# A two-block transformer kernel: SBUF tensors laid out anew, masked_bias apart from the tiles of attention "a"

## The chip, the cores and the metric

One core of one Trainium2 chip. The metric is the device time of one execution in microseconds (us); lower is better.

## The reference

512 tokens of 1,024 features, fp32, pass through two blocks. Block one: RMS norm, one wide projection (`h @ w_in`), windowed grouped-query attention "a" (8 query heads, 2 key heads, window 128, ALiBi slopes and a sink), neighbourhood attention "b" on an 8 x 64 grid with a relative bias, gates, output projection, and an MLP of 4,096 with squared ReLU. Block two has two layers, each a SwiGLU MLP of 2,816, a mixer (sliding-window attention "c" beside a short convolution), and a second SwiGLU MLP. A last RMS norm ends it. For attention "b":

```python
bias = rpb_f[:, dr[:, None, None], dc[None, :, :]]
sc = sc + jnp.transpose(bias, (0, 2, 1, 3))[None]
p = jax.nn.softmax(sc.reshape(b, h, GRID_W, kh * B_KW), axis=-1)
```

and for the MLPs:

```python
x = x + jnp.square(jax.nn.relu(h2 @ w_up[l])) @ w_down[l]          # block one
(jax.nn.silu(h @ w_gate) * (h @ w_up)) @ w_down                     # block two, twice per layer
```

## The kernel before

All activations lie transposed in SBUF, features on the 128 partitions and the 512 tokens along them, in tiles of 2 KB per partition. Each fp32 product is made of three matmuls in fp32r: the high part of the weights by the high part of the activation (L758), high by low (L759), low by high (L760). A weight unit is 128 rows of up to 1,024 columns; three are held (`w_raw`, `w_hi`, `w_lo`). The load queue on SyncE fetches a unit (L1385), ScalarE casts it to `w_hi` (L870), and VectorE (L1066) or, during the attentions, GpSimd (L1305) makes `w_lo`, the rest. A unit feeds eight steps of three matmuls. Results leave PSUM through VectorE into a ring of five `z` tiles, or onto `x`.

A planner writes one list of jobs; each engine walks that list in order and takes its own part of each job, with waits on semaphores between engines. So an engine's queue order is the list's order. Attention steps (score, turn, multiply, turn_out) are set between the dense steps at slots counted by the planner. `split_g` is a weight split on GpSimd, `mask_bias` a job of GpSimd that makes from `rel_bias` the masked bias of attention "b" (affine selects, L1348); VectorE adds it to the scores (L1223). The mask jobs of block 0 stand behind `finish_beside()`, which runs out all steps of attention "a".

SBUF tensors are allocated one after the other in the order of the code, each at a multiple of 32 bytes. Tensors of a stage are allocated on an inner stack and share their space with those of other stages: `act_hi`, `act_lo`, `rms_first` with the mixer's tiles, and within the first mixer the tiles of `part_a` (`ka_hi`, `ka_lo`, `va`) with those of `part_b` (`masked_bias`, `gates_a`). The first tensor of the kernel starts at byte 16,512 of a partition. The small constants come first, then a filler of 256 bytes named `to_page`, so that `x` starts at byte 20,480 (five times 4,096); `h_hi` and `h_lo` (16 KB each), the nine weight buffers (4 KB each), three row sums and the ring follow, then the stages' tiles. Constants in question: `identity` at 16,512, `ones` at 17,024, `dist_1` at 17,536; `dist_2` at 188,448, `masked_bias` at 215,040.

The job and its wait, which the change touches:

```python
pool.wait_ge(in_landed["bias"].s, 16 * BLOCK_C)
if i == 0:
    pool.wait_ge(*done("multiplied", ("a", BLOCKS - 1, 1, len(CHUNKS["a"][BLOCKS - 1]) - 1)))
else:
    pool.wait_ge(*done("biased", ("b", i - 1, g, GROUP - 1)))
```

Of the kernel before, what the change touches and what calls it, by code (L numbers as in the profile page):

```python
# [6 lines left out]
F32 = mybir.dt.float32  # L7
F32R = mybir.dt.float32r
# [4 lines left out]
P = 128  # L13
TOKENS = 512
D_MODEL = 1024
HEAD = 64
HEADS = 8
KV_HEADS = 2
GROUP = HEADS // KV_HEADS
BLOCK = 128  # L20
BLOCKS = TOKENS // BLOCK
KT = D_MODEL // P
# [8 lines left out]
UNIT = KT * P  # L31
UNITS_HELD = 3
Z_RING = 5
# [21 lines left out]
def whole_chunks(windows):  # L55
    return [[(s // BLOCK + c, c * BLOCK, BLOCK) for c in range(n // BLOCK)] for s, n in windows]
# [3 lines left out]
CHUNKS = {"a": whole_chunks(WINDOW_1), "c0": whole_chunks(WINDOW_2), "c1": whole_chunks(WINDOW_2),  # L60
          "b": [[(i, 0, CHUNKS_VB[i][1]), (i + 1, CHUNKS_VB[i][1], CHUNKS_VB[i + 1][1])] for i in range(BLOCKS)]}
# [469 lines left out]
def two_blocks(nc, dram, out):  # L531
    stack = ExitStack()
    with stack:
        def sbuf(name, shape, dt=F32, on=stack):
            return on.enter_context(nc.sbuf_tensor(name, shape, dt))

        def signal(name, step=1):
            return Signal(stack.enter_context(nc.semaphore(name)), step)

        identity = sbuf("identity", [P, P])  # L540
        ones = sbuf("ones", [P, P])
        dist_1 = sbuf("dist_1", [P, 3 * BLOCK])
# [11 lines left out]
        sink_exp = sbuf("sink_exp", [P, 2, HEADS])  # L554
        row_sum = sbuf("row_sum", [P, 2, HEADS])
        row_inv = sbuf("row_inv", [P, 2, HEADS])
        sbuf("to_page", [P, 64])

        x = sbuf("x", [P, KT, TOKENS])
        h_hi = sbuf("h_hi", [P, KT, TOKENS], F32R)  # L560
        h_lo = sbuf("h_lo", [P, KT, TOKENS], F32R)
        w_raw = [sbuf(f"w_raw{i}", [P, UNIT]) for i in range(UNITS_HELD)]
        w_hi = [sbuf(f"w_hi{i}", [P, UNIT], F32R) for i in range(UNITS_HELD)]
        w_lo = [sbuf(f"w_lo{i}", [P, UNIT], F32R) for i in range(UNITS_HELD)]
        scaled_sum = sbuf("scaled_sum", [P, TOKENS])
        rms_inv = sbuf("rms_inv", [P, TOKENS])
        square_sum = sbuf("square_sum", [P, TOKENS])
        z = [sbuf(f"z{i}", [P, TOKENS]) for i in range(Z_RING)]


        with ExitStack() as on:
            act_hi = sbuf("act_hi", [P, FF_RING, TOKENS], F32R, on)
            act_lo = sbuf("act_lo", [P, FF_RING, TOKENS], F32R, on)
            rms_first = sbuf("rms_first", [P, TOKENS], F32, on)
        with ExitStack() as on:
            qa = sbuf("qa", [P, HEADS, TOKENS], F32R, on)
            qb_hi = sbuf("qb_hi", [P, 4, TOKENS], F32R, on)
            qb_lo = sbuf("qb_lo", [P, 4, TOKENS], F32R, on)
            probs_t1 = sbuf("probs_t1", [P, 2, TOKENS], F32, on)
            out_q1 = sbuf("out_q1", [P, TOKENS], F32, on)  # L580
            probs_1 = sbuf("probs_1", [P, 3, GROUP, 3 * BLOCK], F32, on)
            with ExitStack() as kv_part:
                kb_hi = sbuf("kb_hi", [P, 4, TOKENS], F32R, kv_part)
                kb_lo = sbuf("kb_lo", [P, 4, TOKENS], F32R, kv_part)
                vb = sbuf("vb", [P, BLOCKS + 1, HEADS, HEAD], F32, kv_part)
                rel_bias = sbuf("rel_bias", [P, HEADS, 2 * BLOCK], F32, kv_part)
                with ExitStack() as part_a:
                    ka_hi = sbuf("ka_hi", [P, KV_HEADS, TOKENS], F32R, part_a)
                    ka_lo = sbuf("ka_lo", [P, TOKENS], F32R, part_a)
                    va = sbuf("va", [P, BLOCKS, KV_HEADS, HEAD], F32, part_a)  # L590
                with ExitStack() as part_b:
                    masked_bias = sbuf("masked_bias", [P, HEADS, 2 * BLOCK], F32, part_b)
                    gates_a = sbuf("gates_a", [P, 2, TOKENS], F32, part_b)
            with ExitStack() as part_m:
                mg_hi = sbuf("mg_hi", [P, KT, TOKENS], F32R, part_m)
                mg_lo = sbuf("mg_lo", [P, KT, TOKENS], F32R, part_m)
                gates_b = sbuf("gates_b", [P, 2, TOKENS], F32, part_m)
        with ExitStack() as on:
            q2 = sbuf("q2", [P, HEADS, TOKENS], F32R, on)
            k2_hi = sbuf("k2_hi", [P, KV_HEADS, TOKENS], F32R, on)  # L600
            k2_lo = sbuf("k2_lo", [P, TOKENS], F32R, on)
            v2 = sbuf("v2", [P, BLOCKS, KV_HEADS, HEAD], F32, on)
            probs_t2 = sbuf("probs_t2", [P, 2, TOKENS], F32, on)
            out_q2 = sbuf("out_q2", [P, TOKENS], F32, on)
            probs_2 = sbuf("probs_2", [P, 3, GROUP, 2 * BLOCK], F32, on)
            cv_hi = sbuf("cv_hi", [P, 4, TOKENS], F32R, on)
            cv_lo = sbuf("cv_lo", [P, 4, TOKENS], F32R, on)
            conv_c = sbuf("conv_c", [P, TOKENS], F32, on)
            conv_y = sbuf("conv_y", [P, TOKENS], F32, on)
            conv_u = sbuf("conv_u", [P, TOKENS + 2], F32, on)  # L610
            dist_2 = sbuf("dist_2", [P, 2 * BLOCK], F32, on)

        bank = [stack.enter_context(nc.psum_tensor(f"bank{i}", [P, TOKENS], F32)) for i in range(8)]
        dense_bank, score_bank, turn_bank, value_bank = bank[0:4], bank[3:5], bank[5:7], bank[7]
# [15 lines left out]
        done = plan.value  # L630
# [668 lines left out]
        def gpsimd_program(engine):  # L1299
            pool = Once(engine)  # L1300
            for job, key, r, zs in jobs:
# [32 lines left out]
                elif job == "mask_bias":  # L1334
                    i, g = key
                    first, lower, upper = {0: (HALF_BLOCK // GRID_R, (8, 24), (24, 32)), 1: (0, (0, 32), (0, 32)),
                                           3: (0, (0, 8), (8, 24))}[i]
                    heads = lambda t, a, b: t[:, 4 * g:4 * g + 4, :].rearrange("p h (j r) -> p h j r", r=GRID_R)[:, :, a:b, :]
                    pool.wait_ge(in_landed["bias"].s, 16 * BLOCK_C)
                    if i == 0:  # L1340
                        pool.wait_ge(*done("multiplied", ("a", BLOCKS - 1, 1, len(CHUNKS["a"][BLOCKS - 1]) - 1)))
                    else:
                        pool.wait_ge(*done("biased", ("b", i - 1, g, GROUP - 1)))
                    for (a, b), sign, base, event in ((lower, 1, GRID_R - 1, "bias_half"), (upper, -1, (WIN_W - 1) * GRID_R, "bias_masked")):
                        in_place = i == 1 and sign < 0
                        if sign < 0:
                            pool.wait_ge(*done("bias_half", key))
                        engine.affine_select(out=heads(masked_bias, a - first, b - first),  # L1348
                                             in_=heads(masked_bias, a, b) if in_place else heads(rel_bias, a, b),
                                             compare_op=ALU.is_ge, fill=-MASKED, base=base + sign * GRID_R * a,  # L1350
                                             pattern=[[0, 4], [sign * GRID_R, b - a], [0, GRID_R]], channel_multiplier=-sign).then_inc(signals[event].s, 1)

                elif job == "merge_b":
                    m = key
                    pool.wait_ge(*done("merged", m))
                    engine.dma_start(x[:, m, :], dram["x"][m * P:(m + 1) * P, :]).then_inc(x_back[m].s, 16)

                elif job == "conv_h":
                    layer, f = key
                    pool.wait_ge(*done("evacuated", r))  # L1360
                    if f > 0:
                        pool.wait_ge(*done("conv_back_2", (layer, f - 1)))
                    engine.tensor_tensor(conv_u[:, 2:TOKENS + 2], z[zs % Z_RING][:, :], conv_c[:, :], ALU.mult).then_inc(signals["conv_u"].s, 1)

                elif job == "conv_b":
                    pool.wait_ge(*done("evacuated", r))
                    pool.wait_ge(*done("conv_back_2", key))
                    engine.tensor_tensor(z[zs % Z_RING][:, :], z[zs % Z_RING][:, :], conv_y[:, :], ALU.mult).then_inc(signals["conv_out"].s, 1)

                elif job == "output":  # L1370
                    for n, cols in enumerate(halves):
                        pool.wait_ge(signals["inverted"].s, n + 1)
                        for m in output_order:
                            if m < WITH_GAIN:
                                pool.wait_ge(*done("x_gained", m))
                                engine.tensor_tensor(x[:, m, cols], x[:, m, cols], rms_inv[:, cols], ALU.mult).then_inc(signals["output_scaled"].s, 1)
# [181 lines left out]
```

## Time and profile before

| | |
|---|---|
| median of 3 runs | 2581.93 us (2581.85 to 2585.58) |
| profiled execution | 2581.85 us, span 2580.1 us |
| TensorE busy (matmul) | 2543.6 us |
| VectorE, ScalarE, GpSimd busy | 1232.9, 886.2, 276.3 us |
| DMA | 235.36 MB, mean 91 GB/s |

Engines in the rows: PE is TensorE's matmuls, PEld its weight loads, DVE VectorE, ACT ScalarE, POOL GpSimd, SP SyncE. L12 is line 12 of the kernel. Busy time of PE is modelled, since matmuls overlap; the distance between their starts tells the rate. "idle before <- X" is time in which the engine stood still ahead of the instruction, and what ended it.

### The profile page before, as it was taken

The page shows a single profiled execution, that of the slowest core. Times are in us where ns is not written, and L with a number is a line of the kernel's source. Part 1 is how long each engine was busy: PE and PEld are TensorE (multiplying, and loading weights), DVE is VectorE, ACT ScalarE, POOL GpSimd, SP SyncE. Part 2 cuts the span into 40 slices and gives each one's busy share as a digit, 9 for nine tenths or more (in the row PEclk, how much of TensorE's full clock was granted, in tenths as well). Part 3 has the DMA queues.
Part 4 walks back from the last instruction along what each step waited for, and adds up shares of the span by engine and source line. Part 5 has one row for each costly group of instructions (what it writes and reads, how often), then busy time and mean ns, then how long its engine had stood idle before and what let it go on. Part 6 is the DMA issues. An engine that isn't in the chain of part 4 may idle for free.

```text
span 2580.1 us, 28068 instructions
## 1 busy us (share of the span) xinstructions
PE 2543.6 (99%) x11494; PEld 2079.2 (81%) x11494; DVE 1232.9 (48%) x1518; ACT 886.2 (34%) x1329; POOL 276.3 (11%) x194
## 2 busy tenths in 40 slices
PE   7999999999999999999999999999999999999997
PEld 6777888888888888877888888888888778888886
DVE  5444455334465343455454444543434644544444
ACT  4445434223353222344332222422223443322222
POOL 4233110000030000013300000100000132000002
PEclk9999999999999999999999999999999999999999
DMA  5111232333323333231223232333332312233322
GB/s 163 50 50 52 91 116 93 98 99 97 98 83 106 98 98 98 82 100 58 78 94 101 95 98 92 96 98 98 98 98 82 100 59 78 94 100 95 99 94 69
DMA packets 69424, 235.36 MB, mean 91 GB/s; under 512 B 8753, under 2 KB 11441, under 8 KB 69297
## 3 DMA queue, kind: packets, MB, share of 16 engines
q1 hardware_dynamic: 67632, 230.36, 28.2%
q0 software_dynamic: 1664, 3.22, 0.6%
q8 instruction: 91, 1.49, 0.2%
q14 instruction: 37, 0.30, 0.0%
HBM read 231.35 MB, written 2.19 MB: 91 GB/s over the span
## 4 chain that ended last, share of the span: by engine, by line
PE 90%; DVE 4%; ACT 2%; issue 2%; POOL 0%; DMA 0%; SPq 0%; DVEq 0%; ACTq 0%; POOLq 0%
PE bank L758 29%; PE bank L760 28%; PE bank L759 28%; PE bank L772 2%; PE bank L799 2%; DVE w_lo L1066 2%; PE bank L786 1%; ACT w_hi L870 1%; DVE x L1167 1%; ACT z L861 0%; POOL square_sum L1315 0%; DVE q L1123 0%; DVE z L1058 0%; PE bank L810 0%; PE bank L832 0%
## 5 line engine op out<-in xcount | busy, mean ns | idle before, releaser
L758 PE MATMUL bank<-h_hi,w_hi 128*128 128x512 f32 x2224 | 893.0, 402 | 11.2 <-DVE w_lo L1066 9.7
L760 PE MATMUL bank<-h_hi,w_lo 128*128 128x512 f32 x2224 | 869.1, 391 | 0.0
L759 PE MATMUL bank<-h_lo,w_hi 128*128 128x512 f32 x2224 | 868.8, 391 | 0.0
L1066 DVE TENSOR_TENSOR w_lo<-w_raw,w_hi 128x1024 fp32r<-128x1024 f32 (+1 forms) x387 | 483.9, 1251 | 327.0 <-ACT w_hi L870 326.7
L870 ACT ACTIVATE w_hi<-w_raw 128x1024 fp32r<-128x1024 f32 (+1 forms) x438 | 451.9, 1034 | 414.8 <-PE bank L760 412.9
L758 PEld LDWEIGHTS bank<-h_hi,w_hi 128*128 128x128 f32 x2224 | 418.6, 188 | 109.8 <-DVE w_lo L1066 11.2
L760 PEld LDWEIGHTS bank<-h_hi,w_lo 128*128 128x128 f32 x2224 | 418.5, 188 | 88.6
L759 PEld LDWEIGHTS bank<-h_lo,w_hi 128*128 128x128 f32 x2224 | 419.2, 189 | 81.1 <-issue 1.9
L758 PE MATMUL bank<-act_hi,w_hi 128*128 128x512 f32 x960 | 373.9, 389 | 0.0
L760 PE MATMUL bank<-act_hi,w_lo 128*128 128x512 f32 x960 | 373.9, 389 | 0.0
L759 PE MATMUL bank<-act_lo,w_hi 128*128 128x512 f32 x960 | 373.9, 389 | 0.0
L1058 DVE TENSOR_TENSOR z<-bank,rms_inv 128x512 f32<-128x512 f32 x238 | 168.5, 709 | 301.6 <-PE bank L760 300.8
L1315 POOL TENSOR_TENSOR square_sum<-square_sum,z 128x512 f32<-128x512 f32 x62 | 83.9, 1353 | 1853.3 <-ACT z L861 1852.3
L1167 DVE SCALAR_TENSOR_TENSOR x<-bank,x 128x512 f32<-128x512 f32 x152 | 104.7, 689 | 281.8 <-PE bank L760 281.7
L759 PEld LDWEIGHTS bank<-act_lo,w_hi 128*128 128x128 f32 x960 | 180.3, 188 | 37.4
L758 PEld LDWEIGHTS bank<-act_hi,w_hi 128*128 128x128 f32 x960 | 180.2, 188 | 37.4
L760 PEld LDWEIGHTS bank<-act_hi,w_lo 128*128 128x128 f32 x960 | 180.2, 188 | 37.2
L984 ACT ACTIVATE act_hi<-z 128x512 fp32r<-128x512 f32 x88 | 55.6, 632 | 389.6 <-DVE z L1188 389.6
L979 ACT ACTIVATE z<-z 128x512 f32<-128x512 f32 x88 | 55.6, 632 | 285.3 <-DVE z L1058 285.3
L1305 POOL TENSOR_TENSOR w_lo<-w_raw,w_hi 128x1024 fp32r<-128x1024 f32 x51 | 121.9, 2391 | 291.6 <-ACT w_hi L870 291.6
L1066 DVE TENSOR_TENSOR act_lo<-z,act_hi 128x512 fp32r<-128x512 f32 x120 | 83.2, 693 | 105.0 <-ACT act_hi L984 61.4
L1228 DVE SCALAR_TENSOR_TENSOR probs<-dist,bank 128x256 f32<-128x256 f32 (+2 forms) x96 | 40.4, 421 | 109.2 <-PE bank L772 109.2
(163 smaller groups left out, 1666.3 us busy)
## 6 DMA issues: line engine op xcount, KB each, us to landing
w_raw<-ffn_wg_dram SPq DMA_DIRECT2D x88, 512.0 KB, 3.5
w_raw<-ffn_wu_dram SPq DMA_DIRECT2D x88, 512.0 KB, 3.5
w_raw<-w_in_dram SPq DMA_DIRECT2D x70, 512.0 KB, 3.6
w_raw<-ffn_wd_dram SPq DMA_DIRECT2D x64, 512.0 KB, 3.5
w_raw<-w_up_dram SPq DMA_DIRECT2D x32, 512.0 KB, 3.5
w_raw<-w_down_dram SPq DMA_DIRECT2D x32, 512.0 KB, 3.8
w_raw<-w_out_dram SPq DMA_DIRECT2D x24, 512.0 KB, 3.5
w_raw<-ffn_wd_dram SPq DMA_DIRECT2D x32, 384.0 KB, 3.1
```

The lines of the kernel that those rows point to most:

```text
L758: engine.matmul(to, w_hi[s][:, lhs], hi, start=k == 0, stop=False)
L759: engine.matmul(to, w_hi[s][:, lhs], lo, start=False, stop=False)
L760: product = engine.matmul(to, w_lo[s][:, lhs], hi, start=False, stop=job == "k_last")
L772: product = engine.matmul(score_bank[at % 2][:, 0:count], q[:, block(i)], k[:, start:start + count], start=m == 0, stop=m == len(pairs) - 1)
L870: engine.activation(w_hi[s][:, 0:width], w_raw[s][:, 0:width], ACT.Copy).then_inc(signals["w_hi"].s, 1)
L979: engine.activation(z[zs[1] % Z_RING][:, :], z[zs[0] % Z_RING][:, :], ACT.Silu).then_inc(signals["silued"].s, 1)
L984: engine.activation(act_hi[:, plan.hidden[key] % FF_RING, :], z[zs[1] % Z_RING][:, :], ACT.Copy).then_inc(signals["act_hi"].s, 1)
L1058: engine.tensor_tensor(to, src, scale, ALU.mult).then_inc(signals["evacuated"].s, 1)
L1066: engine.tensor_tensor(lo, value, hi.bitcast(F32), ALU.subtract).then_inc(signals[event].s, 1)
L1167: engine.scalar_tensor_tensor(x[:, m, :], dense_bank[plan.results[r].bank][:, :], factor(r), x[:, m, :], ALU.mult, ALU.add).then_inc(signa ...
L1305: engine.tensor_tensor(w_lo[s][:, 0:width], w_raw[s][:, 0:width], w_hi[s][:, 0:width].bitcast(F32), ALU.subtract).then_inc(signals["w_lo_g ...
L1315: engine.tensor_tensor(to, to, z[zs % Z_RING][:, :], ALU.add).then_inc(signals["scaled_sum" if scaled else "square_sum"].s, 1)
```

## The change

Three things change. (1) The tensors that all stages use are allocated first, and the constants behind them; the filler `to_page` is gone, `scaled_sum` moves to the MLP's stage, and in the second mixer `dist_2` stands behind `q2` and `conv_u` ahead of `conv_y`. (2) `masked_bias` moves out of `part_b` and has space of its own beside the tiles of attention "a". (3) The wait of the mask job for the last value product of attention "a" is dropped. All instructions and their order stay; almost all addresses change.

```diff
+        x = sbuf("x", [P, KT, TOKENS])
+        h_hi = sbuf("h_hi", [P, KT, TOKENS], F32R)
+        h_lo = sbuf("h_lo", [P, KT, TOKENS], F32R)
+        w_raw = [sbuf(f"w_raw{i}", [P, UNIT]) for i in range(UNITS_HELD)]
+        w_hi = [sbuf(f"w_hi{i}", [P, UNIT], F32R) for i in range(UNITS_HELD)]
+        w_lo = [sbuf(f"w_lo{i}", [P, UNIT], F32R) for i in range(UNITS_HELD)]
+        rms_inv = sbuf("rms_inv", [P, TOKENS])
+        square_sum = sbuf("square_sum", [P, TOKENS])
+        z = [sbuf(f"z{i}", [P, TOKENS]) for i in range(Z_RING)]
         identity = sbuf("identity", [P, P])
         ones = sbuf("ones", [P, P])
         dist_1 = sbuf("dist_1", [P, 3 * BLOCK])
...
         row_inv = sbuf("row_inv", [P, 2, HEADS])
-        sbuf("to_page", [P, 64])
-
-        x = sbuf("x", [P, KT, TOKENS])
...
-        scaled_sum = sbuf("scaled_sum", [P, TOKENS])
-        rms_inv = sbuf("rms_inv", [P, TOKENS])
-        square_sum = sbuf("square_sum", [P, TOKENS])
-        z = [sbuf(f"z{i}", [P, TOKENS]) for i in range(Z_RING)]
...
             act_lo = sbuf("act_lo", [P, FF_RING, TOKENS], F32R, on)
+            scaled_sum = sbuf("scaled_sum", [P, TOKENS], F32, on)
             rms_first = sbuf("rms_first", [P, TOKENS], F32, on)
...
                 rel_bias = sbuf("rel_bias", [P, HEADS, 2 * BLOCK], F32, kv_part)
+                masked_bias = sbuf("masked_bias", [P, HEADS, 2 * BLOCK], F32, kv_part)
...
                 with ExitStack() as part_b:
-                    masked_bias = sbuf("masked_bias", [P, HEADS, 2 * BLOCK], F32, part_b)
                     gates_a = sbuf("gates_a", [P, 2, TOKENS], F32, part_b)
...
             q2 = sbuf("q2", [P, HEADS, TOKENS], F32R, on)
+            dist_2 = sbuf("dist_2", [P, 2 * BLOCK], F32, on)
...
             conv_c = sbuf("conv_c", [P, TOKENS], F32, on)
+            conv_u = sbuf("conv_u", [P, TOKENS + 2], F32, on)
             conv_y = sbuf("conv_y", [P, TOKENS], F32, on)
-            conv_u = sbuf("conv_u", [P, TOKENS + 2], F32, on)
-            dist_2 = sbuf("dist_2", [P, 2 * BLOCK], F32, on)
...
                     pool.wait_ge(in_landed["bias"].s, 16 * BLOCK_C)
-                    if i == 0:
-                        pool.wait_ge(*done("multiplied", ("a", BLOCKS - 1, 1, len(CHUNKS["a"][BLOCKS - 1]) - 1)))
-                    else:
+                    if i > 0:
                         pool.wait_ge(*done("biased", ("b", i - 1, g, GROUP - 1)))
```

## Rows read from the trace of the kernel before

**Rows 1.** The page: busy us, share of the span, instructions

```profile
PE 2543.6 (99%) x11494; PEld 2079.2 (81%) x11494; DVE 1232.9 (48%) x1518; ACT 886.2 (34%) x1329; POOL 276.3 (11%) x194
```

**Rows 2.** Windows: us, busy us by engine, granted clock, DMA share, GB/s

```profile
0.00:20.00 20.00, 10.27 (x33) 7.40 (x34) 12.54 (x13) 13.63 (x20) 6.23 (x8) 1.00 0.77 279
...
755.00:1080.00 325.00, 325.00 (x1436) 269.18 (x1435) 155.75 (x174) 90.87 (x109) 0.00 (x0) 1.00 0.30 95
```

**Rows 3.** Waits of TensorE, first and last of seven: us, times, longest

```profile
PE bank L758 <- DVE w_lo L1066: 9.7, 3, 8.6
...
PE bank L844 <- ACT z L861: 0.6, 1, 0.6
```

**Rows 4.** Timeline of TensorE in an MLP: start us, us

```profile
904.49 0.39 PE L759 MATMUL bank<-h_lo,w_hi 128*128 128x512 f32 x1
...
905.17 0.39 PE L759 MATMUL bank<-h_lo,w_hi 128*128 128x512 f32 x1
```

**Rows 5.** The page: a group, busy us, mean ns, idle before

```profile
L870 ACT ACTIVATE w_hi<-w_raw 128x1024 fp32r<-128x1024 f32 (+1 forms) x438 | 451.9, 1034 | 414.8 <-PE bank L760 412.9
```

**Rows 6.** Line 759 from 755 to 1080 us: ns min/median/max

```profile
L759 PE MATMUL bank<-h_lo,w_hi x342: 388/390/390, 754.9 to 1073.8; 128*128 128x512 f32 x171
L759 PEld LDWEIGHTS bank<-h_lo,w_hi x341: 187/188/188, 755.3 to 1073.6; 128*128 128x128 f32 x171
...
L759 PE MATMUL bank<-act_lo,w_hi x137: 388/390/390, 846.0 to 1079.9; 128*128 128x512 f32 x137
```

**Rows 7.** Timeline of TensorE at the end of attention "a"

```profile
165.44 0.60 PE L786 MATMUL bank<-identity,probs 128*128 128x128 f32 x4
...
170.69 1.00 PE L799 MATMUL bank<-va,probs_t 128*128 128x64 f32 x8
```

**Rows 8.** Timeline of GpSimd and VectorE around the first mask

```profile
175.93 2.40 POOL L1305 TENSOR_TENSOR w_lo<-w_raw,w_hi 128x1024 fp32r<-128x1024 f32 x1 [5.27 <-ACT w_hi L870]
178.28 4.14 POOL L1348 TENSOR_SCALAR_AFFINE_SELECT masked_bias<-rel_bias 128x512 f32<-128x512 f32 x4
...
180.71 0.36 DVE L1223 SCALAR_TENSOR_TENSOR probs<-bank,masked_bias 128x192 f32<-128x192 f32 x1 [1.83 <-POOL masked_bias L1348]
```

**Rows 9.** Groups by form, score plus masked bias

```profile
L1223 DVE SCALAR_TENSOR_TENSOR probs<-bank,masked_bias 128x256 f32<-128x256 f32 x16 | 6.8, 425 | 24.3 <-PE bank L772 24.3
```

**Rows 10.** Tile dist (dist_1 and dist_2): ns min/median/max

```profile
L1228 DVE SCALAR_TENSOR_TENSOR probs<-dist,bank x96: 286/422/556, 56.8 to 2142.0; 128x256 f32<-128x256 f32 x64, 128x384 f32<-128x384 f32 x16, 128x128 f32<-128x128 f32 x16
```

**Rows 11.** Tile conv_u, the two VectorE lines that read it

```profile
L1205 DVE SCALAR_TENSOR_TENSOR conv_y<-conv_u,conv_w,conv_y x8: 741/744/752, 1163.7 to 2156.3; 128x512 f32<-128x512 f32 x8
L1208 DVE SCALAR_TENSOR_TENSOR conv_y<-conv_u,conv_w,conv_y x8: 752/752/752, 1164.4 to 2157.1; 128x512 f32<-128x512 f32 x8
```

**Rows 12.** Line 832, the norm's product with ones

```profile
L832 PEld LDWEIGHTS bank<-square_sum,ones x16: 185/188/193, 26.0 to 2207.9; 128*128 128x128 f32 x16
L832 PE MATMUL bank<-square_sum,ones x16: 590/594/668, 26.2 to 2208.3; 128*128 128x512 f32 x16
```

**Rows 13.** Timeline in an MLP: a fetch, and the cast that reads it

```profile
898.61 0.33 SPq L1385 DMA_DIRECT2D w_raw<-ffn_wg_dram  x1
...
913.32 1.04 ACT L870 ACTIVATE w_hi<-w_raw 128x1024 fp32r<-128x1024 f32 x1
```

**Rows 14.** DMA issues: count, KB each, median us to landing

```profile
w_raw<-ffn_wg_dram SPq DMA_DIRECT2D x88, 512.0 KB, 3.5
...
w_raw<-ffn_wd_dram SPq DMA_DIRECT2D x32, 384.0 KB, 3.1
...
out_dram<-x SPq DMA_DIRECT2D x8, 256.0 KB, 2.4
...
dist<-dist_dram SPq DMA_DIRECT2D x2, 128.0 KB, 2.1
```

**Rows 15.** Timeline of the start: the third unit's cast

```profile
10.66 1.06 ACT L870 ACTIVATE w_hi<-w_raw 128x1024 fp32r<-128x1024 f32 x1 [0.18 <-DMA w_raw<-w_in_dram]
```

More of the change, by code:

```diff
@@ L556, in two_blocks @@
         row_inv = sbuf("row_inv", [P, 2, HEADS])
-        sbuf("to_page", [P, 64])
-        x = sbuf("x", [P, KT, TOKENS])
[L560 to L564, printed above, removed]
-        scaled_sum = sbuf("scaled_sum", [P, TOKENS])
-        rms_inv = sbuf("rms_inv", [P, TOKENS])
-        square_sum = sbuf("square_sum", [P, TOKENS])
-        z = [sbuf(f"z{i}", [P, TOKENS]) for i in range(Z_RING)]
         with ExitStack() as on:
```

## The prediction

> **What bounds the kernel now.** I read the first two parts of the page first. TensorE is busy 2543.6 us of a span of 2580.1 us, and VectorE, the next engine, is busy 48% [rows 1]. The windows by stage come next: in the second block's stretch of dense matmuls from 755 to 1080 us TensorE is busy 325.00 us of 325.00 at a granted clock of 1.00, so nothing but its own rate counts there, while in the first 20 us it is busy 10.27 us and DMA 0.77 [rows 2]. Then the waits of TensorE: the seven named ones add up to 21.4 us, from 9.7 (the start) down to 0.6 [rows 3]. So there are three places where time can move: TensorE's rate per matmul (some 2,500 us hang on it), these 21 us, and the ends of the kernel, where TensorE has no work.
>
> The rate is the place to look at closely, since the change is mostly one of addresses. Matmuls 0 and 3 of a run start at 904.49 and 905.17 us: 0.68 / 3 = 0.227 us apart [rows 4]. The 438 weight units [rows 5] feed eight steps of three matmuls each, or six steps for the 32 units of 384 KB [rows 14]: 3 x (406 x 8 + 32 x 6) = 10,320 matmuls. The reader is to see that it doesn't matter which operand a matmul reads: over h_lo the model's duration is 388/390/390 ns at least/median/most, over act_lo it is 388/390/390 [rows 6].
>
> **Part 1, the wait that goes.** The mask job of block 0 no longer waits for the last value product of attention "a". That product is the group of eight at 170.69 us, 1.00 us long, so it is over at 171.69 [rows 7]. GpSimd starts the selects at 178.28 us. What stands ahead of them in its queue is a weight split from 175.93 us, 2.40 us long: it ends at 178.33, and the selects begin with no idle time before them [rows 8]. The wait was fulfilled 6.6 us before GpSimd came to it. Taking it away lets nothing start earlier: GpSimd walks its jobs in order, and the job order is the same. I take 0. The lower bound is what a mask at time zero would free: VectorE idles 1.83 us for it, once [rows 8]. So the bounds are -1.8 and 0 us. A loss is excluded, since an instruction that waited for a fulfilled semaphore is only gone.
>
> **Part 2, masked_bias gets its own 8 KB.** Its writers and readers are the same, in the same order. It used to lie on ka_hi, ka_lo and va; now these three move up by 8 KB and gates_a (first written by the gate of tile 0) lies on ka_hi instead. The code already makes that gate wait for the last outputs of "a", which come after every read of ka_hi; that wait stands there before and after the change. If it were ever to bind, the gate behind it would stop ScalarE's casts, which have the 11 us of cover worked out below. 0 us.
>
> **Part 3, scaled_sum, dist_2 and conv_u move within their stages.** No wait in the code is added or taken away for them. dist_2 now lies inside the space of act_hi; its load already waits, in both kernels, for the last matmul of the MLP before. Behind it in the load queue stand weight fetches, as before. 0 us.
>
> **Part 4, every address.** Worked out from the sizes in the code: before, x starts at byte 20,480 of a partition, five times 4,096, and each of h_hi, h_lo, the nine weight buffers, the z ring, act_hi and act_lo starts at a multiple of 2,048. After, x starts at 16,512 = 4 x 4,096 + 128, and h, weights and z lie 128 bytes past such multiples; act_hi starts at 120,576, a multiple of 256 and of no more. The question is whether an engine or a DMA is slower (or faster) for that. The trace of before has operands off the 2,048 grid:
>
> - VectorE: dist_1 lies at 17,536 and dist_2 at 188,448 (128 and 32 past a multiple of 256), masked_bias at 215,040, a multiple of 2,048. A 128x256 scalar-tensor-tensor with one PSUM operand takes 425 ns with masked_bias; the 96 on the two dist tiles have a median of 422 [rows 9, 10]. conv_u is read 4 bytes past its start in 744 ns, at its start in 752 [rows 11]. No price.
> - ScalarE and GpSimd: I have no row for them off the grid and take VectorE's 0. They have cover: ScalarE is idle 414.8 us ahead of the casts [rows 5], GpSimd is busy 11% of the span [rows 1].
> - TensorE weight loads: ones lies at 17,024, 128 past a multiple of 256, exactly where the weights now go. Its loads take 185/188/193 ns; those of the weights on the grid 187/188/188 [rows 6, 12]. No price.
> - TensorE moving operand: no 512-column fp32r operand lies off the grid, so the trace doesn't have this case. The nearest is identity, at 16,512: 128 columns as moving operand of the transposes, four in 0.60 us [rows 7], that is (0.60 - 0.27) / 3 = 0.11 us apart. At the pace of the aligned product with ones (594 ns for 512 columns) [rows 12], 128 columns would take 0.15 us. So no slower than aligned. I take 0, and bound it at half a nanosecond per matmul either way (the spread between 388 and 390 is as large): 10,320 x 0.5 ns = 5.2 us.
> - Weight loads by DMA: a refill is issued at 898.61 us and read by the third cast after that (three slots in turn), at 913.32 us. That leaves 14.7 us for a landing that takes 3.5 us, so 11 us of cover [rows 13, 14]. Of ScalarE's 414.8 idle us ahead of the casts 412.9 end with a matmul, not with a DMA [rows 5]. If that cover were gone, a later landing would be paid on all 438 units.
> - The start, where this cover isn't there: the cast of the third unit begins at 10.66 us, after 0.18 us of waiting for its DMA, and TensorE's first groups wait for such casts and their rests (9.7 us in three waits) [rows 3, 15].
>
> What a DMA to an address off the grid costs: dist_2, 128 KB to 32 past a multiple of 256, lands in 2.1 us. Loads on the grid land in 3.5 us for 512 KB and 3.1 for 384 [rows 14], so 0.4 us per 128 KB, and 128 KB should take 2.3. It takes no more than that. I take 0; the upper bound is one 256-byte piece in sixteen more at the start, 1/16 of 10.66 us = 0.7 us, and at the end a quarter more of the moving part of one 256 KB store, 0.25 x 0.8 = 0.2 us of its 2.4 [rows 14].
>
> The Trainium skill (DMA: Bandwidth & Descriptors, How a descriptor splits into AXI transactions) speaks against this change: a descriptor is cut into 256-byte transactions, and one that doesn't start at a multiple of 256 needs one more. By that rule each 4,096-byte row of a weight buffer would take 17 transactions for 16, if it holds for the side that is written, and the whole change would come to about 2582.8 us. The landing of dist_2 shows no such price for written rows, and the stores at the end, which read x, will show the other side. By it, the weight refills would land some 0.1 us later with no one waiting.
>
> **The sum.** 2581.85 us (the profiled execution, whose span is 2580.1; the median of the three runs is 2581.93) + 0 + 0 + 0 + 0 = 2581.9 us. Below 0.2% of the time, 5.2 us, this kernel's measurement can't tell a change from none: its three runs lie up to 3.7 us apart.
>
> **Rivals.**
> - *The moving operand is streamed at another pace off the grid, slower* (the other side). One cycle more of the 2.4 GHz level per matmul is 0.42 ns x 10,320 = 4.3 us: 2586.2, still "same". It decides from 0.5 ns on; two cycles are 8.6 us: 2590.5 us. For it: this case is in no row, and 512 columns at 2.4 GHz are 213 ns where 227 are spent, so 14 ns have another cause, which may depend on the address. Against it: h_lo, act_lo, and each of their 2 KB-spaced tiles have one pace, and every new start is still a multiple of 128 bytes. 8 in 100.
> - *The same, but faster*: before, weights, x and h all start on the same 4,096 grid, and if part of the 14 ns is engines and DMA meeting at like addresses, spreading them gives some back. 4% of 14 ns = 0.56 ns, 5.8 us: 2576.1 us. Against it: VectorE, ScalarE and DMA come and go beside TensorE, and the pace stays at 0.227. 9 in 100.
> - *The mask wait mattered after all*: 1.8 us less, 2580.1 us, "same". 5 in 100, the queue order excludes it.
> - *DMA off the grid costs at the start and the end*: 0.7 + 0.2 = 0.9 us more, 2582.8 us, "same". 13 in 100.
> - No change anywhere: 65 in 100, the forecast.
>
> **How the numbers follow.** Same: 65 + 5 + 13 = 83 in 100, less 3 for spread between measurements that I give to the two sides: 0.80. Faster 9 + 2 = 0.11, slower 8 + 1 = 0.09. The range takes in the bounds of the hidden costs and the half nanosecond: 2581.9 - 5.2 and 2581.9 + 5.2, rounded, 2577 to 2587 us; about 2 in 10 is left outside.
>
> **What the profile after would show.** If right: spacing of dense matmuls 0.227 us, model durations 390, window of the MLP full; the selects again right behind the split near 175.93 us; weight landings at 3.5 us; the third cast near 10.66 us; VectorE's split still 1.23 us. It would be wrong if the TensorE spacing changed by half a nanosecond, if ScalarE's casts waited for DMA in the MLPs, or if VectorE's or GpSimd's operations got longer by enough that TensorE's 21.4 us of waits grew by a quarter.

## The result, and the profile after

The changed kernel takes 2604.16 us (median of 4 runs, 2604.01 to 2606.43), the kernel before 2583.76 us in the runs beside it (2581.85 to 2586.89). The ratio is 1.008 with a 95% interval of 1.0062 to 1.0097: slower by 0.8%, some 20 us. The prediction said 2581.9 us and no change, with 2577 to 2587 us as its range. The profiled execution took 2604.31 us, span 2602.5 us, 22.4 us over the 2580.1 us of the kernel before.

The page after, part 1 (busy us, share, instructions), answers to [rows 1], and its groups to [rows 5]:

```profile
PE 2567.8 (99%) x11494; PEld 2079.9 (80%) x11494; DVE 1232.8 (47%) x1518; ACT 886.6 (34%) x1329; POOL 276.8 (11%) x194
...
L868 ACT ACTIVATE w_hi<-w_raw 128x1024 fp32r<-128x1024 f32 (+1 forms) x438 | 452.0, 1034 | 431.0 <-PE bank L758 428.4
```

Every engine but TensorE has the busy time that it had, within half a microsecond. TensorE's grew by 24.2 us with the same 11,494 instructions. ScalarE's casts idle more, 431.0 for 414.8 us, and still all but 2.6 us of it ends with a matmul: ScalarE waits longer because TensorE is slower. So the time is in TensorE's own pace, and the groups of the same page say in which matmuls (mean ns behind the busy us):

```profile
L758 PE MATMUL bank<-h_hi,w_lo 128*128 128x512 f32 x2224 | 869.4, 391 | 0.0
L757 PE MATMUL bank<-h_lo,w_hi 128*128 128x512 f32 x2224 | 868.8, 391 | 0.0
...
L758 PE MATMUL bank<-act_hi,w_lo 128*128 128x512 f32 x960 | 379.2, 395 | 0.0
L756 PE MATMUL bank<-act_hi,w_hi 128*128 128x512 f32 x960 | 379.2, 395 | 0.0
L757 PE MATMUL bank<-act_lo,w_hi 128*128 128x512 f32 x960 | 379.1, 395 | 0.0
```

Those that read h have their 391 ns. Those that read act (the tiles `act_hi` and `act_lo`) went to 395 from the 389 that all three groups have on the page before, one of them:

```profile
L759 PE MATMUL bank<-act_lo,w_hi 128*128 128x512 f32 x960 | 373.9, 389 | 0.0
```

The durations are modelled, so the starts have to confirm it. Timeline of TensorE after, in a product with act (start us, us), beside [rows 4]:

```profile
992.15 0.39 PE L756 MATMUL bank<-act_hi,w_hi 128*128 128x512 f32 x1
992.38 0.40 PE L757 MATMUL bank<-act_lo,w_hi 128*128 128x512 f32 x1
992.62 0.39 PE L758 MATMUL bank<-act_hi,w_lo 128*128 128x512 f32 x1
992.85 0.40 PE L756 MATMUL bank<-act_hi,w_hi 128*128 128x512 f32 x1
...
994.95 0.39 PE L756 MATMUL bank<-act_hi,w_hi 128*128 128x512 f32 x1
```

From 992.15 to 994.95 there are 12 matmuls: 0.233 us each, where the kernel before has 0.227. Over all dense matmuls of the trace that follow one another at the upper clock level, the pace on act goes in turns, 229 and 237 ns, one matmul after the other, whatever the operand; the mean from start to start is 233.3 ns (226.7 before), and 227.1 on h in both kernels. All other tensors of a stage (q2, cv, mg, qb) went the way of act: 233.2 ns over all 3,648 matmuls on stage tensors, for 226.8 before. 3,648 x 6.4 ns = 23.3 us, and the loss is 22.4 us.

A small part of the 22.4 us has another cause. Windows of the kernel before, then of the one after (the third number from the end is the granted clock):

```profile
50.00:75.00 25.00, 21.53 (x84) 15.23 (x83) 13.42 (x22) 10.19 (x21) 7.19 (x3) 0.86 0.24 78
50.00:75.00 25.00, 21.52 (x75) 15.10 (x74) 12.38 (x19) 9.70 (x20) 7.21 (x3) 0.80 0.20 65
```

The clock was at its lower level for longer in this execution: 25 us x 0.06 = 1.5 us. It leaves some 21 us for the pace, so the sum of 23.3 us is a little high. The runs below say where such a sum runs high.

The mask, the part of the change that looked like the point of it, did nothing. Timelines of GpSimd and VectorE after, beside [rows 8]:

```profile
177.70 2.40 POOL L1303 TENSOR_TENSOR w_lo<-w_raw,w_hi 128x1024 fp32r<-128x1024 f32 x1 [5.28 <-ACT w_hi L868]
180.05 4.14 POOL L1344 TENSOR_SCALAR_AFFINE_SELECT masked_bias<-rel_bias 128x512 f32<-128x512 f32 x4
...
182.48 0.36 DVE L1221 SCALAR_TENSOR_TENSOR probs<-bank,masked_bias 128x192 f32<-128x192 f32 x1 [1.83 <-POOL masked_bias L1344]
```

The selects stand right behind the split, 2.35 us after its start as before, and VectorE's 1.83 us of waiting is there to the last digit; all is 1.8 us later, most of it the 1.5 us of clock above, which lie ahead of it.

### The profile page after: what moved, and what is told of

It reads as the page before. It is cut to its first block, busy times and chain, and to the rows that moved or that the text cites. A ratio compares the mean times of both kernels' runs of the same rounds, so it can differ in the third digit from the quotient of the medians.

```text
span 2602.5 us, 28067 instructions
## 1 busy us (share of the span) xinstructions
PE 2567.8 (99%) x11494; PEld 2079.9 (80%) x11494; DVE 1232.8 (47%) x1518; ACT 886.6 (34%) x1329; POOL 276.8 (11%) x194
## 4 chain that ended last, share of the span: by engine, by line
PE 92%; DVE 4%; ACT 2%; issue 1%; DMA 0%; POOL 0%; SPq 0%; DVEq 0%; ACTq 0%
PE bank L756 29%; PE bank L758 28%; PE bank L757 28%; PE bank L770 2%; PE bank L797 2%; DVE w_lo L1064 1%; PE bank L784 1%; ACT w_hi L868 1%; DVE x L1165 1%; ACT z L859 0%; DVE q L1121 0%; DVE z L1056 0%; PE bank L808 0%; DMA w_raw<-w_in_dram 0%; PE bank L830 0%
## 5 line engine op out<-in xcount | busy, mean ns | idle before, releaser
L868 ACT ACTIVATE w_hi<-w_raw 128x1024 fp32r<-128x1024 f32 (+1 forms) x438 | 452.0, 1034 | 431.0 <-PE bank L758 428.4
L758 PE MATMUL bank<-act_hi,w_lo 128*128 128x512 f32 x960 | 379.2, 395 | 0.0
L756 PE MATMUL bank<-act_hi,w_hi 128*128 128x512 f32 x960 | 379.2, 395 | 0.0
```

What stands on the lines that cost most here:

```text
L756: engine.matmul(to, w_hi[s][:, lhs], hi, start=k == 0, stop=False)
L758: product = engine.matmul(to, w_lo[s][:, lhs], hi, start=False, stop=job == "k_last")
L868: engine.activation(w_hi[s][:, 0:width], w_raw[s][:, 0:width], ACT.Copy).then_inc(signals["w_hi"].s, 1)
```

## The experiments

The theories, after the result. **O** (own address): a moving operand that starts off some grid streams more slowly. **R** (relation): the pace depends on the distance, the start of the moving operand less that of the weights. Worked out from the layout: before, every moving operand of a dense matmul and every weight buffer start at multiples of 256 bytes, distance 0 modulo 256. After, h is 128 past such a multiple and so are the weights (distance 0), act_hi starts at 120,576 and w_hi at 77,952: distance 42,624 = 166.5 x 256, so 128. What came between them are the 3,712 bytes of constants, 14.5 x 256. **W**: the dropped wait or the separate masked_bias.

**The whole change, with 128 bytes of constants ahead of x.**

```diff
+        gate_bias = sbuf("gate_bias", [P, 2 * KT])
+        eps_col = sbuf("eps_col", [P, 1])
+        root_ready = sbuf("root_ready", [P, 1])
         x = sbuf("x", [P, KT, TOKENS])
...
         dist_1 = sbuf("dist_1", [P, 3 * BLOCK])
-        eps_col = sbuf("eps_col", [P, 1])
-        root_ready = sbuf("root_ready", [P, 1])
...
-        gate_bias = sbuf("gate_bias", [P, 2 * KT])
```

> The whole change, but with 128 bytes of constants put ahead of x, so that x, h, the weights and z start 256 bytes past a multiple of 512, as the stage tensors (act_hi, act_lo, q2, cv, mg) do in the changed kernel. The stage tensors keep their addresses. Theory R (relation: the pace of a matmul depends on where its moving operand and the weights start relative to each other): all matmuls at 0.227 us, about 2582 us. Theory O (own address: a moving operand that starts 256 past a multiple of 512 is slow by itself): act stays at 233 ns and h joins it, 10,320 x 6.6 ns = 68 us over the kernel before, about 2650 us. Theory W (the dropped wait or the separate masked_bias did it): 2604 us as the changed kernel.

Measured: ratio to the kernel before 1.0001 (0.9991 to 1.001), median 2588.04 beside 2587.48 us (that the kernel before stands at 2587 us here, and at 2584 above, goes with the clock: see the last section). act keeps the very addresses that it has in the changed kernel and runs at the pace of before. Its groups:

```profile
L757 PE MATMUL bank<-h_lo,w_hi 128*128 128x512 f32 x2224 | 869.6, 391 | 0.0
L756 PE MATMUL bank<-act_hi,w_hi 128*128 128x512 f32 x960 | 373.4, 389 | 0.0
L757 PE MATMUL bank<-act_lo,w_hi 128*128 128x512 f32 x960 | 373.4, 389 | 0.0
```

W falls: the wait is gone, masked_bias is apart, and nothing is slower. O falls. R stands.

**256 bytes ahead of the stage tensors of the kernel before.**

```diff
         z = [sbuf(f"z{i}", [P, TOKENS]) for i in range(Z_RING)]
+        sbuf("to_stage", [P, 64])
```

> The kernel before with 256 bytes of filler ahead of the stage tensors: weights and h on the grid, act and the other stage tensors 256 past a multiple of 512; wait and masked_bias as before. Theory O: act at 233 ns, h at 226.7, some 2604 us. Theory R: act slow too, by an amount that depends on the distance (256 here, 128 in the changed kernel); fast only if distances count modulo 256. Theory W: 2582 us, no change.

Measured: ratio 0.9998 (0.9986 to 1.001), act 226.7 ns from start to start. Distance 256 costs nothing.

**512 bytes for 256 ahead of x in the kernel before.**

```diff
-        sbuf("to_page", [P, 64])
+        sbuf("to_page", [P, 128])
```

> The kernel before with a filler of 512 bytes for 256 ahead of x: x, h, weights, z and all stage tensors are 256 past a multiple of 512. Theory R: everything at 226.7 ns, 2582 us. Theory O: all 10,320 dense matmuls at 233 ns, about 2650 us. Theory W: 2582 us.

Measured: ratio 1.0001 (0.9991 to 1.001), h 227.1 and the stage tensors 226.8 ns. O expected 68 us and got none.

**128 bytes ahead of the stage tensors of the kernel before**: the same line as for 256, with 32 columns. This is the distance of the changed kernel and nothing else of it.

> The kernel before with 128 bytes of filler ahead of the stage tensors: weights on the grid, stage tensors 128 past it, the distance that the changed kernel has. Theory R: stage matmuls at 233 ns, in turns 229 and 237, about 2604 us. Theory O: h ran at 227 ns at 128 past the grid in the changed kernel, so 226.7 ns here and 2582 us. Theory W: 2582 us.

Measured: ratio 1.009 (1.0074 to 1.0106), 2610.9 beside 2587.48 us, 23.4 us. Groups:

```profile
L760 PE MATMUL bank<-h_lo,w_hi 128*128 128x512 f32 x2224 | 870.8, 392 | 0.0
L759 PE MATMUL bank<-act_hi,w_hi 128*128 128x512 f32 x960 | 379.2, 395 | 0.0
L760 PE MATMUL bank<-act_lo,w_hi 128*128 128x512 f32 x960 | 379.1, 395 | 0.0
```

act has the 395 ns of the changed kernel and its turns of 229 and 237 ns. One filler of 128 bytes makes the whole loss.

**128 bytes between h_lo and w_raw in the kernel before**: the weights and all behind them move.

```diff
+        sbuf("to_weights", [P, 32])
         w_raw = [sbuf(f"w_raw{i}", [P, UNIT]) for i in range(UNITS_HELD)]
```

> The kernel before with 128 bytes of filler between h_lo and w_raw: x and h stay on the grid, weights, z and all stage tensors lie 128 past it. Theory R (distance between moving operand and weights, modulo 256): now the matmuls that read h are slow, 233 ns, and those that read act are fast, 226.7; 6,672 x 6.6 ns = 44 us, about 2631 us beside 2587 of the kernel before on this chip. Theory S (the stage tensors must lie on the phase of x and h, or on the grid): act slow and h fast, about 2610 us.

Measured: ratio 1.0139 (1.01 to 1.0178), 33.6 us more. The slow and the fast group have changed places:

```profile
L760 PE MATMUL bank<-h_lo,w_hi 128*128 128x512 f32 x2224 | 880.3, 396 | 0.0
...
L760 PE MATMUL bank<-act_lo,w_hi 128*128 128x512 f32 x960 | 373.5, 389 | 0.0
```

h hasn't moved and is slow, act has moved and is fast. From start to start h takes 233.0 ns, 5.9 more: 6,672 x 5.9 = 39 us, for the 44 expected. The span of the profiled execution is 39.3 us longer than before, but some 5 of them are the clock (granted 0.80 for 0.86 from 50 to 75 us, and 0.93 for 1.00 from 1145 to 1195 us), so the pace costs some 34 us, and the sum is high here too.

**128 bytes ahead of w_lo and 128 behind it**: w_lo alone is off.

```diff
+        sbuf("to_low", [P, 32])
         w_lo = [sbuf(f"w_lo{i}", [P, UNIT], F32R) for i in range(UNITS_HELD)]
+        sbuf("past_low", [P, 32])
```

> The kernel before with 128 bytes of filler ahead of w_lo and 128 behind it: w_lo alone lies 128 past the grid. Theory R1 (a matmul is slowed by the load of the NEXT weights, which runs while it streams): of each three matmuls only L759, under which w_lo is loaded, is slow, by some 6.6 ns; 3,440 x 6.6 = 23 us, about 2610 us. Theory R2 (a matmul's own weights count): only L760, which uses w_lo, is slow, and by the same sum. If it is not weights against moving operand at all but x, z or the stage tensors among themselves: no change, 2587 us.

Measured: ratio 1.0129 (1.0089 to 1.017), 31 us. Neither R1 nor R2 alone. In this kernel L760 is the first of the three matmuls, L761 the one under which w_lo is loaded, L762 the one that uses it:

```profile
L760 PE MATMUL bank<-act_hi,w_hi 128*128 128x512 f32 x960 | 373.4, 389 | 0.0
...
L761 PE MATMUL bank<-act_lo,w_hi 128*128 128x512 f32 x960 | 380.2, 396 | 0.0
L762 PE MATMUL bank<-act_hi,w_lo 128*128 128x512 f32 x960 | 381.1, 397 | 0.0
```

Both neighbours of the odd load pay: from start to start 226.7, 232.5 and 234.2 ns on act, and the same on h. The two together are 13.2 ns per k-step; 3,440 x 13.2 = 45 us would be the sum, and the span shows 36.4 us more (2616.5 for 2580.1), or some 38 at the clock of before (0.93 for 0.86 from 50 to 75 us). The medians, 31 us apart, set two executions with a granted clock of 0.997 and 0.996 against ten of which nine have 0.993 or 0.994. The loss is smaller beside attention: of the 10,320 dense matmuls, numbers 300 to 1,000 lose 1.7 us, 2.4 ns each, and 1,400 to 4,000, nearly all in MLPs, 10.8 us, 4.2 ns each. So a sum over all matmuls runs high, in the other kernels too where dense matmuls stand beside attention.

**64, 32, 192 and 96 bytes ahead of the stage tensors**, each the line of the 256 run with another width, to see which distances cost.

> The kernel before with 64 bytes of filler ahead of the stage tensors: distance 64. If the cost stands for every distance that is not a multiple of 256, act is at 233 ns and the time some 23 us above the kernel before. If it grows with the distance up to 128: half, 230 ns and 12 us. If only bit 7 of the address counts (128 or not): 226.7 ns and no change.

> The same with 32 bytes: distance 32. If every distance that is not a multiple of 256 costs the same: 233 ns, 23 us. If it grows with the distance: 228.4 ns, 6 us. If only bit 7 counts: no change.

> 192 bytes of filler ahead of the stage tensors of the kernel before: distance 192, which is -64 modulo 256. If the cost depends on the size of the distance either way, as at 64: 229.0 ns in the mean on act and some 5 to 8 us more. If 64 was cheap for another reason: up to 233 ns and 23 us.

> 96 bytes of filler: distance 96. 32 and 128 gave a mean of 233.3 ns on act, 64 gave 229.0. If 64 is an exception: 233 ns and 23 us. If the cost falls towards 64 from both sides: between 229 and 233 ns.

Measured, the mean from start to start on all stage tensors, and the ratio to the kernel before (distance in bytes, modulo 256; 256 as built):

| distance | ns | ratio (95%) |
|---|---|---|
| 0 (before) | 226.8 | |
| 32 | 233.3 | 1.0076 (1.0054 to 1.0099) |
| 64 | 229.0 | 1.0022 (1.0011 to 1.0033) |
| 96 | 233.4 | 1.0097 (1.0062 to 1.0132) |
| 128 | 233.2 | 1.009 (1.0074 to 1.0106) |
| 192 | 233.3 | 1.0082 (1.0044 to 1.0119) |
| 256 | 226.8 | 0.9998 (0.9986 to 1.001) |

Neither "it grows with the distance" nor "192 is as cheap as 64" held. Each of the five distances tried that are no multiple of 256 costs, four of them the same 6.5 ns, and 64 a third of it. The direction counts: 192 is 64 short of 256, and costs in full. The three matmuls share it differently; at 64 the mean on act is 394, 388 and 392 ns for L759, L760, L761:

```profile
L759 PE MATMUL bank<-act_hi,w_hi 128*128 128x512 f32 x960 | 378.3, 394 | 0.0
L761 PE MATMUL bank<-act_hi,w_lo 128*128 128x512 f32 x960 | 376.4, 392 | 0.0
L760 PE MATMUL bank<-act_lo,w_hi 128*128 128x512 f32 x960 | 372.6, 388 | 0.0
```

**128 bytes between act_hi and act_lo**: one moving operand alone is off.

```diff
             act_hi = sbuf("act_hi", [P, FF_RING, TOKENS], F32R, on)
+            sbuf("to_low", [P, 32], F32, on)
             act_lo = sbuf("act_lo", [P, FF_RING, TOKENS], F32R, on)
```

> The kernel before with 128 bytes of filler between act_hi and act_lo: weights, h and act_hi on the grid, act_lo alone 128 past it, so that of the 3 x 960 matmuls on act only the 960 of L759 stream an operand at distance 128 from all weights. In the kernel with w_lo alone moved, both the matmul under which w_lo was loaded (232.5 ns) and the one that used it (234 ns) were slow. Theory P (moving operand against its own and the next weights): only L759 slow, 7 to 13 ns more, 7 to 12 us over the kernel before. Theory C (each change of phase from one read of TensorE to the next costs, weights loads and streams in turn): L759 and L758 or L760 slow, 13 ns for the three together, some 13 us. If only the weights' own places count: no change.

Measured: ratio 1.0023 (1.0002 to 1.0043). L760 is the one that streams act_lo here:

```profile
L760 PE MATMUL bank<-act_lo,w_hi 128*128 128x512 f32 x960 | 379.2, 395 | 0.0
L759 PE MATMUL bank<-act_hi,w_hi 128*128 128x512 f32 x960 | 373.4, 389 | 0.0
L761 PE MATMUL bank<-act_hi,w_lo 128*128 128x512 f32 x960 | 372.5, 388 | 0.0
```

Theory P: 234.2 ns for the odd one, 226.7 and 225.8 for its neighbours, 6.6 ns for the three together, 960 x 6.6 = 6.3 us. Theory C wanted a second slow matmul, and there is none. The six runs of this kernel lie between 2587.82 and 2598.59 us, so the ratio alone would say little; the pace says it. Beside the w_lo run this says who is the pair. An odd weight load slows the stream ahead of it and the one behind; an odd stream slows only itself. So what counts is a stream against the weights on either side of it, its own and the next.

## Why the prediction was wrong

- **What bounds the kernel** was right, and "the rate is the place to look at closely" too. TensorE's waits stayed small (the first, 9.7 us before, is 9.4).
- **Part 1, the wait**: right. Fulfilled 6.6 us early, nothing to free; the run with the whole change at distance 0 shows wait and masked_bias at 1.0001.
- **Parts 2 and 3**: right by the same run.
- **Part 4, VectorE, weight loads on their own, DMA of the weights**: right. VectorE on dist has a median of 421 ns for 422 [rows 10], the matmuls on h, with weights and h both at 128, keep 227.1 ns, the weights land in 3.5 us. ScalarE and GpSimd, taken at 0 without a row, have the busy time of before.
- **Part 4, TensorE's moving operand**: this step failed. I took 0 and bounded it at half a nanosecond per matmul; it was 6.4 ns on 3,648 of them. Two things were wrong in it. The row that I leaned on, the transposes with identity, has no bearing: they start 108 or 109 ns apart in every run, with identity at distances 0, 32, 64, 96, 128 and 192 from the probabilities. The product with ones that I set beside them as aligned [rows 12] wasn't either: square_sum at 110,592 and ones at 17,024 are at distance 128. In the changed kernel they are at 0, and the median is 591 ns for 594. So two pairs of fp32 operands stood at distance 128 in the kernel before and show no price, and the fp32r matmuls do. And I asked of each tensor alone whether it is off the grid. I wrote down that h and the weights lie 128 bytes past a multiple of 256 and that act_hi is such a multiple, and didn't subtract the one from the other: the constants had moved in between, so that the stage tensors no longer lie at the distance to the weights that they had. By their own addresses those were the safe ones, and they are the slow ones. No row of a dense matmul of before could have shown its price, since all of them have distance 0 modulo 256. That could have widened the bound: a relation that is the same in every row isn't tested by any of them.
- **The rival "another pace, slower"** had the engine and the sign. It had the wrong matmuls (all 10,320, by their own address) and a size of 4 to 9 us; the runs showed 3,648 matmuls by distance, and 6.4 ns. It had 8 in 100. What I held against it, "every new start is still a multiple of 128 bytes", is the very number at which it costs. And the view that h_lo and act_lo have one pace [rows 6] said only that both had the same distance.
- **DMA at the ends**: the store of 256 KB out of x took 2.6 us for 2.4 [rows 14], the 0.2 us that I gave as the bound. With x back at a multiple of 256, in the first experiment, it is 2.4 again, as in every other kernel run. The issues view of the changed kernel (count, KB, median us to landing):

```profile
out_dram<-x SPq DMA_DIRECT2D x8, 256.0 KB, 2.6
```

This read side agrees with the rule of the Trainium skill cited in the prediction (DMA: Bandwidth & Descriptors, How a descriptor splits into AXI transactions); the loads, which write off the grid, keep 3.5 us and don't show it to the 0.1 us of the view.

What stays open is the mechanism inside TensorE: why a stream is slower when its start and that of its own or the next weights differ modulo 256 bytes, why the fp32 transposes don't pay, why 64 costs a third and 192 all, and why 128 goes in turns of 229 and 237 ns. The runs show the rule, not its cause. The Trainium skill (SBUF — State Buffer, SBUF: two separate sides) says that PE never waits on anyone at its SBUF ports, and the same page (A bandwidth-pool intuition that's wrong (but worth ruling out)) has, in its table, a second, independent read port for weight loads. The dense matmuls on act have no idle time ahead of them in any run (0.0 in the groups above), which agrees. But that its two reads can be looked at one by one, as I did, doesn't hold: how they lie to each other costs 6.4 ns of 227, and the measurement decides. Whether the ports are where it arises, no run shows.

## What to carry to other kernels

Treat the layout of SBUF as part of a matmul kernel's tuning: keep moving operands and weight tiles at the same offset modulo 256 bytes, and check it whenever a small constant is moved between them; the absolute offset (128, or 256 past a multiple of 512) cost nothing here. This is shown for fp32r matmuls of 512 columns with weights loaded for each; other types weren't run, and fp32 transposes pay nothing. When a change moves addresses, list pairs that are read at the same time, not tensors one by one, and don't bound a price by rows that all share the property in question. If a kernel bound by TensorE gets slower with no new wait, compare the distance between starts of matmuls by operand before anything else.

Of the kernels run, none beats the one before. The whole change with 128 bytes of constants ahead of x gives the separate masked_bias at no cost, and needs no filler.

## What was not expected of the hardware

Besides the distance rule: single runs of one kernel came at about 2582 or at 2587 us and over. The profiled execution of the first experiment (2587.54 us) shows where 5 us go. Windows: us, busy us by engine, granted clock, DMA share, GB/s; first this experiment,

```profile
1145.00:1170.00 25.00, 22.97 (x86) 17.23 (x85) 9.62 (x24) 9.17 (x20) 8.53 (x4) 0.80 0.20 63
```

then the kernel before:

```profile
1145.00:1170.00 25.00, 22.96 (x106) 17.52 (x104) 11.37 (x25) 11.66 (x28) 11.12 (x6) 1.00 0.25 80
```

In the same 25 us TensorE got through 86 matmuls for 106: a clock of 0.80 there is some 10 us at 1.2 for 2.4 GHz, and costs 5 us. Ahead of it TensorE had stood idle 2.03 us for VectorE in that mixer, and 2.04 us at the same place in the kernel before, where the clock stayed up. So the same idle time is followed by the lower level in some executions and not in others. Of the 25 runs of the kernel before that stand beside the first four experiments, those near 2582 us have a mean granted clock of 0.996, and those from 2586 us on 0.993 or 0.994, hence their median of 2587.48 us. Differences of a few microseconds between kernels have to be read past it, as the distance between starts allows.
